# Two of four convolution blocks moved into the attention rounds of a two-block transformer kernel, and weight pieces spread over the rounds

## What is computed

```python
qk = conv(concat(q, k), conv_w, width 5, per channel); qk = silu(qk)   # 512 channels = 4 blocks of 128
y_mlstm = scan(q, k, v, log_i, log_f) forwards + backwards, 4 heads of 64, times sigmoid(o)
y_attn  = softmax(rope(rmsnorm(aq)) rope(rmsnorm(ak))^T / 8) av        # 8 heads, 2 key heads
y_pool  = (window means - u) @ pool_w * scale
x = x + concat(y_pool, y_mlstm, y_attn) @ w_out
x = x + cross_attention(rmsnorm(x), mem);  x = x + moe(rmsnorm(x))     # 16 experts, 32 tokens each
```

## Time and profile before

| what | us |
|---|---|
| median of 3 runs | 1497.78 |
| lowest, highest run | 1495.62, 1498.93 |
| the profiled execution's own time | 1495.81 |
| its span (first to last instruction) | 1494.0 |
| busy PE / DVE / ACT / POOL | 1156.1 / 443.3 / 379.1 / 69.3 |

### The profile page before, as it was taken

How to read it: one execution, slowest core, us unless ns; L and a number is a source line. 1 busy time by engine, 2 the same in 40 slices (tenths; PEclk the granted TensorE clock), 3 DMA queues, 4 the chain that set the end, 5 groups by cost and what they waited for, 6 DMA issues and landing times.

```text
span 1494.0 us, 20251 instructions
## 1 busy us (share of the span) xinstructions
PE 1156.1 (77%) x8876; PEld 779.3 (52%) x8876; DVE 443.3 (30%) x879; ACT 379.1 (25%) x836; POOL 69.3 (5%) x83
## 2 busy tenths in 40 slices
PE   9999999999998997897556567566665665675677
PEld 8998989999976875442223223223222232232234
DVE  5555777545678854010000000000000000000002
ACT  5655566444555644110000000000000000000002
POOL 0000020000033411000000000000000000000000
PEclk9999999999998998898778787877777787877888
DMA  8435546555553388999999999999999999999996
GB/s 316 166 138 202 197 170 233 204 198 198 198 179 119 104 341 362 376 434 441 426 437 429 431 434 433 436 431 430 436 427 440 425 438 429 434 433 432 428 421 275
DMA packets 29164, 503.37 MB, mean 337 GB/s; under 512 B 4114, under 2 KB 4754, under 8 KB 8084
## 3 DMA queue, kind: packets, MB, share of 16 engines
q1 hardware_dynamic: 25200, 493.43, 79.4%
q10 hardware_dynamic: 3876, 8.65, 1.7%
HBM read 501.02 MB, written 1.05 MB: 336 GB/s over the span
## 4 chain that ended last, share of the span: by engine, by line
issue 63%; PE 31%; DVE 3%; ACT 2%; POOL 1%; DMA 0%; POOLq 0%; DVEq 0%; ACTq 0%
PE PB L99 30%; PE PB L102 1%; DVE SPL L108 1%; ACT SPH L105 1%; POOL SPL L108 0%; DVE XN L116 0%; DVE AQK L108 0%; DMA RAW<-in_wst_dram 0%; POOL SM L136 0%; POOL SP L112 0%; ACT XN L105 0%; DVE SM L128 0%; ACT SP L105 0%; DVE XQL L108 0%; DVE RT L108 0%
## 5 line engine op out<-in xcount | busy, mean ns | idle before, releaser
L99 PE MATMUL PB<-RING,XS 128*32 128x512 f32 x2048 | 297.6, 731 | 173.8 <-DMA RING<-in_wgu_dram 170.0
L99 PEld LDWEIGHTS PB<-RING,XS 128*32 128x32 f32 x2048 | 69.3, 128 | 347.3 <-DMA RING<-in_wgu_dram 185.2
L99 PE MATMUL PB<-RING,HHT 128*32 128x256 f32 x2048 | 152.3, 456 | 108.9 <-DMA RING<-in_wdn_dram 106.6
L108 DVE TENSOR_TENSOR SPL<-RAW,SPH 128x512 fp32r<-128x512 f32 x316 | 209.0, 719 | 42.3 <-ACT SPH L105 40.1
L99 PE MATMUL PB<-XTH,SPL 128*128 128x256 f32 x704 | 201.7, 287 | 0.0
L99 PE MATMUL PB<-XTH,SPH 128*128 128x256 f32 x704 | 199.2, 283 | 0.0
L99 PE MATMUL PB<-XTL,SPH 128*128 128x256 f32 x704 | 199.1, 283 | 0.0
L105 ACT ACTIVATE SPH<-RAW 128x512 fp32r<-128x512 f32 x340 | 186.8, 621 | 12.1 <-DMA RAW<-in_wst_dram 5.3
L99 PEld LDWEIGHTS PB<-RING,HHT 128*32 128x32 f32 x2048 | 72.2, 130 | 173.7 <-DMA RING<-in_wdn_dram 110.6
L105 ACT ACTIVATE SG<-PB 128x512 f32<-128x512 f32 (+1 forms) x21 | 11.9, 566 | 510.0 <-PE PB L99 508.7
L99 PEld LDWEIGHTS PB<-XTL,SPH 128*128 128x128 f32 x704 | 135.0, 192 | 0.5
(11 more groups left out here) (315 smaller groups left out, 1353.7 us busy)
## 6 DMA issues: line engine op xcount, KB each, us to landing
RAW<-in_wst_dram SPq DMA_DIRECT2D x84, 1024.0 KB, 4.8
RING<-in_wgu_dram SPq DMA_DIRECT2D x13, 2048.0 KB, 40.5
RING<-in_wgu_dram SPq DMA_DIRECT2D x14, 1024.0 KB, 9.0
RING<-in_wdn_dram SPq DMA_DIRECT2D x6, 2048.0 KB, 13.5
RING<-in_wgu_dram SPq DMA_DIRECT2D x2, 4096.0 KB, 19.5
RING<-in_wdn_dram SPq DMA_DIRECT2D x2, 4096.0 KB, 17.9
RING<-in_wdn_dram SPq DMA_DIRECT2D x3, 1024.0 KB, 42.8
RAW<-in_wst_dram SPq DMA_DIRECT2D x4, 256.0 KB, 5.6
```

What stands on the lines that cost most here:

```text
L99: return pe.do(lambda e: e.matmul(out_, lhsT, rhs, start=start, stop=stop), after)
L108: return on.do(lambda e: e.tensor_tensor(out_, a, b, op), after)
```

## The change

- Ahead of the rounds, the `bg(4, 2)` behind the gates' running sums and the one behind the rotary go, and the one between them becomes `bg(2, 2)`. `conv` is split in two parts (the taps; the tanh and the last step), and the caller decides where each stands. Blocks 0 and 2 come first: taps behind the first tile of UP and MV, the rest behind `turn_qk(1)`, with a `bg(4, 2)` behind them.
- Blocks 1 and 3 move into rounds 0 and 1: taps behind `ca_memory`, the rest ahead of the closing `bg`.
- Rounds 1 to 3 get a `bg(1)` behind `attn_turn`; `bg(4, 1)` at the end becomes `bg(1, 1)` (rounds 0 and 1) or `bg(3, 1)` (rounds 2 and 3) behind `ca_memory` and `bg(3, 1)` at the end.
- SP_ moves to 151.5, 153.5, 175.5 and 127 kB (dead tensors of the rotary), the exponentials no longer wait for block 3, and the fills of the ring's places wait for other readers.
- Expert 2's first two parts of 4 MB are loaded one by one, each when expert 1's part there is read. The first expert's gathers are issued one step further ahead.

```diff
--- before.py
+++ after.py
@@ -242,7 +242,7 @@
     BC = place("BC", [P, T], F32, at(194))
     MS = place("MS", [P, T], F32, at(195))
     NAC = place("NAC", [P, 2, P], F32, at(196))
-    SP_ = [place(f"SP{i}", [P, 512], F32, at(135 + 2 * i)) for i in range(4)]
+    SP_ = [place(f"SP{i}", [P, 512], F32, at(kb)) for i, kb in enumerate((151.5, 153.5, 175.5, 127))]
     ST_ = [place(f"ST{i}", [P, 512], F32, at(119 + 2 * i)) for i in range(4)]
 
     CQ = place("CQ", [P, 4, T], F32, at(119))
@@ -851,6 +851,7 @@
     s_r = [sem(f"s_r{i}") for i in range(NS // 2)]
     s_fill = {}
     s_second = [sem(f"s_second{i}") for i in range(4 * NS)]
+    s_third = [sem("s_third0"), sem("s_third1")]
     s_half = [sem(f"s_half{i}") for i in range(2 * NS)]
     s_end = [sem(f"s_end{i}") for i in range(5)]
     chunk_in, chunk_at = [None] * NCHUNK, [None] * NCHUNK
@@ -873,7 +874,7 @@
         note(0, g, q, n, [load(sp, RING[slot][:, c], weights_of(0, g)[:, c], s_fill[first], 16, *after)])
 
     def ring_load(e, j, after):
-        token = load(sp, PAIR[SLOT_OF[2 * j] // 2][:, :], io["wgu"][2 * e + j] if j < 2 else io["wdn"][e], s_r[j], 16 * (e - 1), after)
+        token = load(sp, PAIR[SLOT_OF[2 * j] // 2][:, :], io["wgu"][2 * e + j] if j < 2 else io["wdn"][e], s_r[j], 16 * (e - 1 - (j == 0)), after)
         note(e, 2 * j, 0, 4, [token])
         note(e, 2 * j + 1, 0, 4, [token])
 
@@ -881,6 +882,10 @@
         slot = SLOT_OF[g]
         c = slice(UNIT * q, UNIT * (q + n))
         note(1, g, q, n, [load(sp, RING[slot][:, c], weights_of(1, g)[:, c], s_second[4 * g + q], 16, after)])
+
+    def ring_third(g, after):
+        slot = SLOT_OF[g]
+        note(2, g, 0, 4, [load(sp, RING[slot][:, :], weights_of(2, g), s_third[g], 16, after)])
 
     def ring_half(g, h, after):
         slot = SLOT_OF[g]
@@ -907,6 +912,9 @@
         elif e == 0:
             if q == 3:
                 ring_second(g, 0, 4, w)
+        elif e == 1 and g < 2:
+            if q == 3:
+                ring_third(g, w)
         elif e < 14:
             if q == 3 and g % 2:
                 ring_load(e + 1, g // 2, w)
@@ -1090,21 +1098,21 @@
         for j in range(1, 5):
             c = [stt(CO[:, b, :], CI[:, b, j:j + T], CW[:, b, j:j + 1], CO[:, b, :], ALU.mult, ALU.add, ci)
                  for b, ci in zip(bs, c)]
+        yield
         a = [act(QK[:, b, :], CO[:, b, :], ACT.Tanh, ci, ffn_done, scale=0.5) for b, ci in zip(bs, c)]
         for b, ai in zip(bs, a):
             qk_ok[b] = stt(QK[:, b, :], QK[:, b, :], 1.0, CO[:, b, :], ALU.add, ALU.mult, ai)
+        yield
 
     conv_product(0)
     bg(4, 2)
     conv_product(1)
     m1, m2, mt = next(gates)
-    bg(4, 2)
     turn_qk(0, r0, (2, 3))
     conv_product(2)
     conv_product(3)
-    bg(4, 2)
+    bg(2, 2)
     r1 = next(rot1)
-    bg(4, 2)
 
 
     def turn_gates():
@@ -1126,10 +1134,12 @@
         mv_ok.append(m)
         if t == 0:
             nac, em = turn_gates()
-            conv((0, 1))
+            heads01 = conv((0, 2))
+            next(heads01)
     xt_read = w
     turn_qk(1, r1, (2, 3))
-    conv((2, 3))
+    next(heads01)
+    bg(4, 2)
 
     ct = {}
 
@@ -1185,7 +1195,7 @@
         e = []
         for j in range(2):
             pr = SP_[2 * (i % 2) + j]
-            e += [act(pr[:, t * T:t * T + T], PB[bs[j]][:, t * T:t * T + T], ACT.Exp, d, st.get(("tr", i - 2)), qk_ok[3],
+            e += [act(pr[:, t * T:t * T + T], PB[bs[j]][:, t * T:t * T + T], ACT.Exp, d, st.get(("tr", i - 2)),
                       scale=0.125, bias=nm[:, 2 * j + t:2 * j + t + 1], accum_out=rs[:, 2 * j + t:2 * j + t + 1])
                   for t in range(2)]
         held[bs[0]] = held[bs[1]] = e
@@ -1305,12 +1315,21 @@
         scan_scores(i)
         if i >= 1:
             attn_turn(i - 1)
+            bg(1)
         attn_norm(i, pool if i < 3 else dve)
         scan_weights(i)
         ca_memory(i)
+        if i < 2:
+            late = conv((1 + 2 * i,))
+            next(late)
+            bg(1, 1)
+        else:
+            bg(3, 1)
         if i >= 1:
             scan_values(i - 1)
-        bg(4, 1)
+        if i < 2:
+            next(late)
+        bg(3, 1)
     og = [stt(MO[:, t, :], MO[:, t, :], 1.0, NG[:, :], ALU.add, ALU.mult, mo_ok[t], c2_in) for t in range(2)][-1]
 
     def w_out2(t, n, ks):
@@ -1363,7 +1382,7 @@
 
 
     ring_fill(16, 2, unit_free[uv + 1])
-    for i, after in ((18, st["read", 3]), (13, st["tr", 3]), (14, st["values", 3]), (15, st["pv", 3]), (19, scan_end)):
+    for i, after in ((13, qk_ok[3]), (14, st["values", 3]), (18, st["tr", 3]), (15, st["pv", 3]), (19, scan_end)):
         ring_fill(i, 1, after)
 
     w_out2(1, 1, range(2))
@@ -1725,10 +1744,11 @@
     MS3 = small(8).rearrange("p (t i) -> p t i", t=2)
     eps_ok = fill(MS3[:, :, 3:4], EPS)
     gather_first(0)
+    gather_first(1)
     for k in range(KD):
         w = expert_in(0, k)
-        if k + 1 < KD:
-            gather_first(k + 1)
+        if k + 2 < KD:
+            gather_first(k + 2)
     cols_ok = row_columns()
     gather(1)
     for e in range(16):
```

## The result

The changed kernel takes 1502.69 us (median of 13 runs, 1499.67 to 1504.32) against 1497.29 for the kernel before beside it (13 runs): a ratio of 1.0038, interval 1.003 to 1.0047. It is slower, by 5.4 us. Part of that lies ahead of the change: the first running sum of the gates, which the change doesn't touch, starts at 455.66 after and at 454.43 before. I take these 1.23 us off where I compare times of the two traces, and call such a time aligned.

A forecast was written before the change was run, and what follows sets the result against it. Expert weights on the DMA bound the kernel, so the end follows the first refill. Terms -9.6 + 3.0 + 3.9 + 4.3 + 2.8 = +4.4 at the rounds' end gave a refill about +4 later: 1501.8 us, range 1495 to 1506.

The forecast's parts named there:

- the middle piece: Rounds 1 to 3, ahead of the reciprocal: VectorE waits for ACT's high part, reciprocal 2.8 us later each round.
- The front: Stretch ahead of the rounds: less VectorE work, so round 0 starts at 474.0 instead of 483.56, -9.6 us.
- Round 0: First round: block 1's taps, tanh wait, last step and POOL contention add 3.0 us, 7.95 becomes 10.9.
- Rounds 1 and 2: Middle piece in both, block 3 in round 1, more low parts and POOL contention in round 2: +3.9 and +4.3 us.
- Behind the rounds: After round 3: PE waits for VectorE until 523.8, then runs solid to the matmuls that started at 525.40 before.
- The first refill: Expert stage's first ring refill, issued at 600.02 before: about 4 us later, bounds +1 and +7.
- Rival A: Rounds: PE sets them, the new piece's wait is slack; faster, 1493 to 1495.4 us; chance 0.17.
- Rival C: Expert stage, 600 to 610 us: the DMA's lost 2.7 us come back in full, 1499 us; chance 0.15.
- Rival B: Rounds 0 and 1: POOL's normalisation holds up VectorE's lone taps at the shared port, +10, 1508 us; chance 0.10.

The follow-up runs named there:

- experiment 1: Changed kernel with the single middle piece of rounds 1 to 3 moved to the pieces behind `ca_memory`: 1497.53 us, 1.0005 to the kernel before.
- experiment 11: Middle piece put back in rounds 1 to 3 of a 1491.05 us variant without it and with eight pieces behind the rounds: 1496.12 us, 1.0001.
- experiment 4: Changed kernel with the attention normalisation on VectorE in all rounds, none on POOL: 1505.31 us, 1.0061 to the kernel before.
- Experiments 6 and 7: Changed kernel with 14 or 8 unread dummy matmuls on PE ahead of head 3's read-out: 1503.96 us (1.0053) and 1502.01 us (1.0044).
- experiment 2: Kernel before with only the two edits of the expert stage: 1497.14 us, 1.0005 to the kernel before.
- experiment 5: From experiment 1, POOL's four low parts of rounds 0 and 1 given to VectorE: 1497.14 us, 1.0005 to the kernel before.
- experiment 12: Changed kernel without middle piece, all four blocks ahead of the rounds as before, eight of the front's pieces in the rounds: 1494.53 us, 0.9987.

## Why the prediction was right, and where it was off

The sign, the time (1501.8 against 1502.69) and the cause were right: the rounds start early, longer rounds give that back, and the middle piece is the loss on top. Taking that piece out saves 4.9 us (experiment 1), putting it into a faster kernel costs 5.1 (experiment 11). By its steps:

- *The front.* Forecast 474.0 for the first maxima, measured 474.85, aligned 473.6, at a granted clock of 1.00. Right, with two misses that cancel: the second running sum took 1.40 us where before it took 2.66, so the rotary began 1.1 us sooner (aligned), and its first step took 1.80 instead of 0.81, beside POOL's pieces, which were to be through by then and ran until 463.71.
- *The middle piece.* Forecast a wait of some 2.9 us ahead of one low part, three times; measured 3.02 three times. Right, and with it the reciprocal, at 6.4 us behind the maxima instead of 3.6.
- *Round 0.* Forecast 10.9, measured 13.34. This term was mis-sized by 2.4: I allowed 0.8 for two POOL pieces beside low parts and nothing beside other steps. The 128x4 step took 1.0 more, the last step of block 1 0.8 more. The taps took 2.86 (480.66 to 483.52) instead of 2.2: a lone tap is 0.56 in after and 0.51 without POOL beside it (experiment 4), not the 0.46 that I estimated. The low parts came within 0.1 of what I allowed.
- *Rounds 1 and 2.* Forecast 14.2 and 12.8, measured 15.05 and 11.44. In round 1 the step on 128x128 took 1.20 (0.47 in before), beside a POOL piece. In round 2 none of the contention that I booked (0.8) came. The rest of the 1.4 lies mostly in two small terms: the added low part cost 0.4 instead of 0.67, as before's three (2.08) were themselves a little longer than three alone (1.90), and the step behind the reciprocal starts 0.09 us after it instead of 0.32, since the exponential that it waits for is long done. So round 2's miss took off more than half of what round 0's had put on.
- *Behind the rounds.* The forecast has PE wait for VectorE until 523.8 and then "solid and stays so" to the attention values, at before's 6.0 us. That step failed, for the clock behind the wait: PE had waited 2.22 us, and the stretch took 7.71. Experiments 6 and 7 give 6.0 with the wait filled, so 1.7 us of clock were missing in the sum.
- *The first refill.* Forecast +4 (bounds +1 and +7), aligned +7.4, so just outside its bounds. The misses of the steps add up to that: -0.3 in the front, +2.4, +0.9 and -1.4 in the rounds, +1.9 from round 3 to the refill. The median moved by 5.4 only. The runs of before scatter over 7 us and those of after over 5, so one pair of profiled executions doesn't settle these 2 us; that the total came closer to the forecast than the refill did is in part luck.
- *Rival A* (PE binds, the wait is slack) falls: removing the wait gave 4.9 us. The prediction says that PE's waits in rounds 1 and 2 are for POOL and VectorE; the longest of them, 1.03 us at 507.47 in before, is for ACT, which changes nothing here. *Rival C* falls as a mechanism for after (1.0005 in experiment 2; 327 GB/s behind the first refill in after, where it had asked for 400), though a quarter of it showed in experiment 2. *Rival B* named the right resource and the wrong work. The Trainium skill ("SBUF — State Buffer", section "SBUF: two separate sides") has a VectorE instruction with two SBUF inputs and a GpSimd instruction that reads SBUF exclude each other, the later one waiting in full. For POOL's low parts, with two SBUF inputs, the trace agrees: VectorE's step ends with POOL's or up to 0.6 us behind it. For the normalisation it does not agree: four taps 2.24 us beside it, 2.05 without; and three low parts, which the prediction calls unhindered at 2.14, take 1.90 without (485.07 in experiment 5). The 128x4 step and VectorE's normalisation in experiment 4 were held by POOL's low parts too, and they have one SBUF input, not two.

What the change was worth part by part: the edits of the expert stage nothing that can be told; the middle piece +5 us; the rest together as good as nothing (experiment 1: 1.0005). The new places of SP_ and the new readers of the fills were not tried alone. The blocks in the rounds bring no gain of their own either: with the same distribution of pieces they stand at 0.9967 in the rounds and at 0.9958 ahead of them. What did make the kernel faster is eight of the front's pieces behind the rounds instead of ahead of them. The rounds then start 6.1 us sooner with the same 16 pieces in them (483.6 to 477.4 in the table), and the first refill comes 5.1 us sooner. Put into the rounds instead, the same eight pieces take most of it back: there PE waits for VectorE (1.43 us at 499.01, 1.07 at 510.41 in the trace of experiment 12). Taken out of before's rounds, eight pieces bring nothing: there VectorE waits for PE, which began late. That these waits are the reason is read from the traces, not tested by itself.

## What to carry to other kernels

A piece of background work isn't priced by its duration but by when its input is ready on the other engine: ahead of an in-order queue's critical step, a piece of 0.7 us brought a wait of 3.0 each time, because its first half stood behind four instructions on ACT; three such waits cost 5 us of the total. Work handed to POOL is free for VectorE only if none of the steps that it holds runs beside it; count the holds before the hand-over. And where two engines are close behind each other, work that leaves one stretch has to leave the next one too: the same eight pieces were worth 0.13% moved into the rounds and 0.42% moved behind them.

## What the runs showed of the hardware

- POOL's low part (two operands in SBUF, 128x512) held even the smallest steps on VectorE: a tensor_scalar on 128x4 with one operand in SBUF took 1.15 us instead of 0.17, a scalar_tensor_tensor on 128x256 1.21 instead of 0.42, a tensor_tensor on 128x128 1.20 instead of 0.29. The maxima, which read PSUM, took 1.28 us beside it and 1.27 alone. POOL's tensor_scalar, also in SBUF, cost four taps only 0.19 us in all.
- VectorE's low parts lengthen POOL's steps in turn: POOL's four normalisation steps of round 2 in after took 5.22 us beside four of them, 4.00 in round 0.
- After a wait of 2.22 us, PE's next stretch took 7.71 instead of 6.0 us, though its granted clock had been 1.00 (2.4 GHz) for the 16 us before; the stretch began at a mean of 0.70. Fillers of 1.95 us in that wait held it at 1.00 and 6.04 us.
